# One inference step of a hybrid decoder: the query latents and the pool inputs of the front stage as seven half products per pair instead of eight

## What is computed

```
h = rms_norm(x, attn_norm)
z = h @ w_in                 # 2048 -> q_a 512 | ckv 256 | krope 64 | u 512 | qm 512 | gate 2048
q_a, ckv, krope, u, qm, gate = split(z)
kv = rms_norm(mem) @ w_mem_kv                       # 256 memory tokens -> 1024
mla   = attend(rms_norm(q_a) ..., rms_norm(ckv), rope(krope))   # prompt: causal; sample: paged cache
pool  = (mean of the last 2 / 4 / 8 / 16 rows of u, minus u) @ w_pool * pool_scale
cross = softmax(qm k) v
x = x + (concat[mla, pool, cross] * silu(gate)) @ w_out;  y = rms_norm(x)
```

## Time and profile before

| | before |
|---|---|
| median of 3 runs | 867.82 us (867.19 to 867.97) |
| profiled execution, span from first to last instruction | 865.3 us |
| profiled execution's own time | only its span is recorded; the median is 2.5 us above it |
| PE busy | 856.4 us (99%) |
| DVE / ACT / POOL busy | 590.4 / 464.5 / 147.4 us |
| DMA | 168.56 MB, mean 195 GB/s |

### The profile page before, as it was taken

One profiled execution on the slowest core, in us unless ns is written; L12 is line 12 of the kernel. 1 busy time (PEld: TensorE's weight loads), 2 busy tenths in 40 slices (PEclk: granted clock), 3 DMA queues, 4 the chain that ended last, 5 costly groups with the idle time before them and its releaser, 6 DMA issues.

```text
span 865.3 us, 15858 instructions
## 1 busy us (share of the span) xinstructions
PE 856.4 (99%) x5549; PEld 781.2 (90%) x5549; DVE 590.4 (68%) x1018; ACT 464.5 (54%) x774; POOL 147.4 (17%) x210
## 2 busy tenths in 40 slices
PE   9999999999999999999999999999999999999996
PEld 9999999999989999999999999888887788888885
DVE  6546635532349688888888875967678889563777
ACT  7665422122233566676667663577777546363446
POOL 0003001411300112323232331000000111111123
PEclk9999999999999999999999999999999999999998
DMA  9895435223364587878788754524127775988586
GB/s 357 303 290 208 134 134 182 73 85 103 102 256 182 175 275 245 253 256 248 250 254 251 250 172 136 220 86 159 37 97 299 165 213 115 257 218 262 118 156 218
DMA packets 64878, 168.56 MB, mean 195 GB/s; under 512 B 9672, under 2 KB 27657, under 8 KB 62808
## 3 DMA queue, kind: packets, MB, share of 16 engines
q1 hardware_dynamic: 52672, 126.46, 42.4%
q0 software_dynamic: 10752, 33.56, 16.9%
q10 hardware_dynamic: 1376, 7.54, 2.5%
...
## 4 chain that ended last, share of the span: by engine, by line
PE 99%; ACT 0%; issue 0%; DVE 0%; POOL 0%; ACTq 0%; DVEq 0%; POOLq 0%
...
## 5 line engine op out<-in xcount | busy, mean ns | idle before, releaser
L67 PE MATMUL z<-x_hi,w_hi 128*128 128x288 f32 x512 | 152.5, 298 | 0.0
L69 PE MATMUL z<-x_hi,w_lo 128*128 128x288 f32 x512 | 150.8, 294 | 0.0
L68 PE MATMUL z<-x_lo,w_hi 128*128 128x288 f32 x512 | 150.7, 294 | 0.0
L184 ACT ACTIVATE w_hi<-w_raw 128x1024 fp32r<-128x1024 f32 (+2 forms) x62 | 64.8, 1045 | 135.7 <-PE z L69 55.0
L191 DVE TENSOR_TENSOR w_lo<-w_raw,w_hi 128x1024 fp32r<-128x1024 f32 (+2 forms) x62 | 76.9, 1241 | 70.8 <-ACT w_hi L184 70.4
L1024 POOL DMA_DIRECT2D v_raw<-in_cache x128 | 69.3, 541 | 176.0 <-issue 174.4
L67 PEld LDWEIGHTS z<-x_hi,w_hi 128*128 128x128 f32 x512 | 96.1, 188 | 2.7 <-issue 1.1
L68 PEld LDWEIGHTS z<-x_lo,w_hi 128*128 128x128 f32 x512 | 96.1, 188 | 1.6 <-issue 0.2
L69 PEld LDWEIGHTS z<-x_hi,w_lo 128*128 128x128 f32 x512 | 96.0, 188 | 0.0
L2056 ACT ACTIVATE o_hi<-o_raw 128x1024 fp32r<-128x1024 f32 x50 | 52.9, 1060 | 71.1 <-PE pa_s L3030 38.1
L2310 DVE TENSOR_TENSOR o_lo<-o_raw,o_hi 128x1024 fp32r<-128x1024 f32 x50 | 60.9, 1220 | 34.6 <-ACT o_hi L2056 34.4
...
## 6 DMA issues: line engine op xcount, KB each, us to landing
w_raw<-in_w_feat SPq DMA_DIRECT2D x56, 512.0 KB, 4.0
k_raw<-in_cache SPq DMA_DIRECT2D x128, 192.0 KB, 3.1
v_raw<-in_cache POOLq DMA_DIRECT2D x128, 128.0 KB, 3.3
o_raw<-in_w_out POOLq DMA_DIRECT2D x30, 512.0 KB, 8.4
o_raw<-in_w_out SPq DMA_DIRECT2D x20, 512.0 KB, 8.5
w_raw<-in_w_mem_kv SPq DMA_DIRECT2D x16, 512.0 KB, 4.3
...
```

What stands on the lines that cost most here:

```text
L67: pe.matmul(out, a[0], b[0], start=start, stop=False, skip_group_check=onto)
L68: pe.matmul(out, a[0], b[1], start=False, stop=False, skip_group_check=onto)
L69: return pe.matmul(out, a[1], b[0], start=False, stop=stop, skip_group_check=onto)
L184: act.activation(hi_slot(s, u)[:, lo:w], s.wraw[:, u % RAW, lo:w], ACT.Copy).then_inc(s.w_hi, 1)
```

## The change

The eight tiles of q_a and u are taken out of the ring of units and computed ahead of the memory units, as four pairs of tiles. For a pair the product is a 2 x 2 by 2 x 2 product of blocks: two feature tiles by two halves of the inputs, times two halves of the inputs by two halves of the tokens. Directly that takes eight half products; the change uses seven (a form of Strassen's scheme), each of 24 matmuls of 288 columns, on sums of blocks. With a, b, c, d the four weight blocks of 128 x 1024 of a pair, the weight sums are X = c + d, Y = X - a, Z = b - Y and a - c; of x scaled by the norm's weights (`x_scaled`, four blocks f0 to f3 of 128 x 2304) the token sums are T1 = f1 - f0, T2 = f3 - T1, T3 = f3 - f1 and T4 = f2 - T2. The products are, in this order: X T1, Y T2, Z f3, (a - c) T3, a f0, d T4, b f2; their sums are put together by three copies on ACT and six additions on DVE for each pair.

- POOL, new: 13 instructions of 128 x 576 that make `x_scaled` (L494 of the changed kernel), while x arrives, and T3 (L500). ACT makes the other three tiles' upper blocks.
- DVE, new: T1, T2, T4 (L807, L811, L819), the low parts of T1 to T4 (L770), four weight sums for each pair (L721 to L748), the low part for each product (L763), the six additions.
- ACT, new: the high parts of T1 to T4 (L570) and of the weights of each of 28 products (L588), three ahead of PE.
- Then units in the order `ORDER`: the four pool gates' tiles and one tile of qm (numbered 0 to 4, units f0 to f9), mixed with the memory units m0 to m15. Before, two memory units and one feature unit alternated, and the gates came last.
- The work of the pool group moves into this stretch; at which unit each step stands is written in tables (`DIFF_AT`, `PO_AT`, `BEND_AT` and others, by the unit's place in `ORDER`).
- The later filling has 60 parts instead of 64 (the tile of qm went to the front); `LONG` loses the steps 6, 12, 18 and 24.

```diff
-FEATS, FRONT = 28, 12
+PGATE, GATE, QM = range(0, 4), range(5, 17), (4, 17, 18, 19)
+FEATS, FRONT = 20, 5
 BASE = KV_UNITS + MEM_UNITS
...
+FIRST = BASE + 2 * FRONT
...
+ORDER = [("f", 0), ("f", 1), ("m", 0), ("m", 1), ("m", 2), ("m", 3)]
+for n_ in range(2, 8):
+    ORDER += [("f", n_), ("m", 2 * n_), ("m", 2 * n_ + 1)]
+ORDER += [("f", 8), ("f", 9)]
...
+PAIRS, TERMS = 4, 7
+PRODUCTS = PAIRS * TERMS
...
+TERM_ROLE = "XYZcadb"
...
+ACT_F = 13
...
+Z_OUT_AT = {4: 0, 12: 1, 18: 2, 24: 3}
+DIFF_AT = {6: 0, 12: 1, 16: 2, 20: 3}
+PO_AT = {12: 0, 16: 1, 20: 2, 24: 3}
+BEND_AT = {9: 0, 16: 1, 19: 2, 25: 3}
+POOLED_AFTER = {9: 0, 13: 1, 17: 2, 20: 3}
...
+            for n in range(1, PAIRS):
+                done = TERMS * (n - 1)
+                if n == 1:
+                    sp.wait_ge(s.w_used, KV_UNITS)
+                else:
+                    sp.wait_ge(s.st_used, done)
+                sp.wait_ge(s12, 2 * n - 1)
+                pair_load(n, "c")
+                sp.wait_ge(s.st_used, done + 1)
+                pair_load(n, "d")
+                sp.wait_ge(s.st_used, done + 2)
+                pair_load(n, "a")
+                sp.wait_ge(s.st_used, done + 3)
+                pair_load(n, "b")
...
+            pool.wait_ge(gx0_in, 16)
+            for c, (k0, k1) in enumerate(X_CHUNKS):
+                pool.wait_ge(xt_landed[c], 16)
+                for k in range(k0, min(k1, ACT_F)):
+                    pool.tensor_scalar(fs[:, 2 * (k // 8):2 * (k // 8) + 2, k % 8, :], halves(xraw[:, k, :]), gx[:, k:k + 1], None,
+                                       ALU.mult).then_inc(scaled, 1)
...
+            pool.wait_ge(scaled, ACT_F)
+            pool.wait_ge(x_hi, 2 * KD - ACT_F)
+            pool.wait_ge(x_lo, KD)
+            pool.tensor_tensor(traw[:, 2, :, :], fs[:, 3, :, :], fs[:, 1, :, :], ALU.subtract).then_inc(s3, 1)
...
+                pool.wait_ge(u_ready, 3 * (g + 1))
...
+                pool.tensor_copy(by_seq(U(g))[:, :, 0:STATE], src).then_inc(prep, 1)
+                pool.wait_ge(prep, 2 + 2 * (g + 1))
+                if g:
                     pool.wait_ge(diff, g)
-                cur, nxt, other = U[:, g, :], s0, s1
...
+                v = gt[:, g, :]
                 pool.tensor_tensor(po[:, g, :], po[:, g, :], v, ALU.mult).then_inc(gated, 1)
                 pool.wait_ge(gated, 2 * g + 1)
                 pool.tensor_tensor(v, po[:, g, :], th[:], ALU.mult).then_inc(gated, 1)
...
+            def turned_hi(t):
+                if t != 3:
+                    act.wait_ge(t_sum, {1: 1, 2: 2, 4: 3}[t])
+                if t in (2, 3):
+                    act.wait_ge(s3, 1)
+                act.activation(t_high(t), traw[:, t - 1, :, :], ACT.Copy).then_inc(st_hi, 1)
...
+            def pair_hi(m):
...
+                if m < HI:
+                    act.wait_ge(s.w_used, m + 4)
+                else:
+                    act.wait_ge(s.st_used, m - HI + 1)
+                act.activation(high(s, m % HI), raw(n, role), ACT.Copy).then_inc(st_hi, 1)
...
+            turned_hi(1)
+            pair_hi(0)
+            square_row(0)
+            turned_hi(2)
+            pair_hi(1)
+            turned_hi(3)
+            pair_hi(2)
+            turned_hi(4)
...
+            for step in range(PRODUCTS):
+                n, i = divmod(step, TERMS)
...
+                        act.wait_ge(bc, 1)
+                        act.wait_ge(s.st_used, 22 - TERMS)
+                    name, dst = {0: ("C", target(n, 1, 1)), 1: ("B", target(n, 0, 1)), 4: ("A", target(n, 0, 0))}[i]
+                    act.activation(dst, sums_bank(n, name), ACT.Copy).then_inc(st_cp, 1)
+                if step + HI < PRODUCTS:
...
+                if j in BEND_AT:
+                    g = BEND_AT[j]
+                    act.wait_ge(z_out, g + 1)
                     if g:
                         act.wait_ge(gated, 2 * g)
-                    act.activation(th[:], gt[:, g % GT, :], ACT.Sigmoid).then_inc(bent, 1)
+                    act.activation(th[:], gt[:, g, :], ACT.Sigmoid).then_inc(bent, 1)
...
+            def first(n):
...
+                dve.tensor_tensor(raw(n, "X"), raw(n, "c"), raw(n, "d"), ALU.add).then_inc(s12, 1)
...
+            def second(n):
...
+                dve.tensor_tensor(raw(n, "Y"), raw(n, "X"), raw(n, "a"), ALU.subtract).then_inc(s12, 1)
...
+            def third(n):
...
+                dve.tensor_tensor(raw(n, "c"), raw(n, "a"), raw(n, "c"), ALU.subtract).then_inc(s3, 1)
...
+            def fourth(n):
...
+                dve.tensor_tensor(raw(n, "Z"), raw(n, "b"), raw(n, "Y"), ALU.subtract).then_inc(s4, 1)
...
+            def pair_lo(m):
...
+                if k == 12:
+                    dve.wait_ge(scaled, 8)
+                    dve.tensor_tensor(traw[:, 0, :, :], fs[:, 1, :, :], fs[:, 0, :, :], ALU.subtract).then_inc(t_sum, 1)
+            dve.wait_ge(scaled, ACT_F)
+            dve.wait_ge(x_hi, 2 * KD - ACT_F)
+            dve.wait_ge(t_sum, 1)
+            dve.tensor_tensor(traw[:, 1, :, :], fs[:, 3, :, :], traw[:, 0, :, :], ALU.subtract).then_inc(t_sum, 1)
+            first(0)
+            turned_lo(1)
+            second(0)
+            pair_lo(0)
+            fourth(0)
+            third(0)
+            dve.wait_ge(t_sum, 2)
+            dve.tensor_tensor(traw[:, 3, :, :], fs[:, 2, :, :], traw[:, 1, :, :], ALU.subtract).then_inc(t_sum, 1)
+            turned_lo(2)
+            pair_lo(1)
+            pair_lo(2)
+            turned_lo(3)
...
+                    dve.wait_ge(s.w_used, gate_unit(g) + 1)
...
+                    dve.tensor_tensor(halves(gt[:, g, :]), gate_sums, rbc[:], ALU.mult).then_inc(z_out, 1)
+                if j in PO_AT:
+                    g = PO_AT[j]
                     dve.wait_ge(pooled, g + 1)
...
+                if j in DIFF_AT:
+                    g = DIFF_AT[j]
                     dve.wait_ge(win, (g + 1) * (g + 2) // 2)
                     sm = (s0, s1)[g % 2]
                     if g:
                         dve.wait_ge(pooled, g)
...
+            def pair_product(m):
+                n, i = divmod(m, TERMS)
+                turned = {0: 1, 1: 2, 3: 3, 5: 4}
+                if i in turned:
+                    b = t_high(turned[i]), t_low(turned[i])
...
+                    b = {2: x_block(8, 1), 4: x_block(0, 0), 6: x_block(8, 0)}[i]
+                bank, start = {0: ("C", True), 1: ("B", True), 2: ("C", False), 3: ("B", False), 4: ("A", True), 5: ("B", False), 6: ("C", True)}[i]
...
+                pe.wait_ge(st_hi, hi_count(m))
+                pe.wait_ge(st_lo, lo_count(m))
+                w = high(s, m % HI), low(n, TERM_ROLE[i])
+                for kk in range(8):
+                    last = product(pe, sums_bank(n, bank), [v[:, P * kk:P * kk + P] for v in w],
+                                   (b[0][:, kk, :], b[1][:, kk, :]), start and kk == 0, kk == 7, not start)
+                last.then_inc(s.st_used, 1)
...
-LONG = (*range(2, 28, 2), STEPS - 1)
+LONG = (2, 4, 8, 10, 14, 16, 20, 22, 26, STEPS - 1)
...
+            dve.tensor_tensor(s.qm[:, 0, :].rearrange("p (a b) -> p a b", a=2), s.front_sums, rbc[:], ALU.mult).then_inc(qm0_out, 1)
...
```

771 lines of the change are left out of this document (462 added, 309 removed).

## The result

The changed kernel takes 884.23 us (median of 4 runs, 881.42 to 885.22) against 867.76 us (4 runs): 1.0187 times as long, 95% interval 1.0171 to 1.0203, or 16.5 us more. The profiled execution is the shortest of them, 881.42 us with a span of 879.7, so its trace accounts for 14.4 us only. The last experiment shows where most of the other 2.8 us sit.

A forecast was written before the change was run, and what follows sets the result against it. PE, busy 99% of the span, was taken to bound the kernel. 867.8 - 12.8 (matmuls saved) + 22 (start) + 8.5 (second sigmoid) + 3 (clock) = 888.5 us; range for 8 in 10, 868.5 to 898.

The forecast's parts named there:

- Saved on PE: Four pairs at the front: seven half products instead of eight, 96 matmuls less at 0.133 us each, 12.8 us gained.
- Added on DVE at the start: DVE's row of sums and low parts before the first two products: 8.3 us to each, 5.1 us of waiting as lower bound.
- POOL in DVE's way: At the start, 13 scalings (1.2 us each, 15.6) and T3 (4.45) add to DVE's time: second product at 64.8, 22 us lost.
- The second sigmoid: Ahead of m10, ACT's sigmoid waits for POOL's first gate, behind group 3's four window additions: 8.5 us lost, 7 to 10.
- The clock: PE waits longer than 4 us two or three times and restarts at a lower clock: 3 us for all, 0 to 6.
- The filling: Four of the 38 steps lose a part of 3.2 us; DVE still short of full: nothing, up to 3 us.
- The sum: Whole kernel: 867.8 - 12.8 + 22 + 8.5 + 3 = 888.5 us.
- Rival 1: At the start, POOL does not hold DVE up, scalings fall into DVE's gaps or leave the port free: 870.1 us, chance 0.15.
- Rivals 2 and 3: 2: the sigmoid's wait costs nothing, 880.0 us, chance 0.12; 3: only DVE's row waits at the second product, 860.1, chance 0.10.
- the gap at m10: Sign of being right: an 8 us gap on PE ahead of m10, released through ACT's w_hi behind the sigmoid.
- rival 4: On PE, more matmuls run than counted, not the seven products; PE's instruction list has 95 rows less; chance 0.01.
- the gaps of 10 and 5 us at the start: Sign of being right: PE gaps of some 10 and 5 us ahead of the first two half products.

The follow-up runs named there:

- The last experiment: The changed kernel run once more as it is, on the same chip, nothing changed: 884.13 us, ratio 1.0183; the profiled run took 884.85 us.

## Why the prediction was right and wrong

It said 888.5 us, in a range of 868.5 to 898, slower with 0.86; measured are 884.2. The direction and the mechanism hold: two chains on other queues, one at the start and one ahead of m10, and a clock that falls behind them. By its own steps:

- **Saved on PE**, 12.8 us: 96 matmuls went (5549 to 5453). The front ends 24.7 us late and the kernel 14.4, so 10.3 us of it arrive.
- **Added on DVE at the start**: right to 0.1 us an instruction (2.46 us for 2304 columns, 1.14 for 1024). From T2 to the second product the row and T3 were to take 16.7 + 4.45 = 21.2 us and took 22.3.
- **POOL in DVE's way**: here the prediction failed, by 8.5 us. The second product was put at 64.8 us and started at 56.35, so 13.5 us were lost and not 22. The step that failed is the price of a scaling as seen by VectorE: 1.2 us was taken, fully added to VectorE's time, and it was 0.42 us (0.46 by the run with three fewer), though the instruction itself takes 2.16 us on GpSimd. 13 x 0.42 = 5.4 us in place of 15.6 puts T2 at 28.0 + 5.4 = 33.4 us; it was at 34.08. I took a one-input instruction to shut VectorE out for as long as it runs, as a two-input one does. For the two-input T3 that is nearly what happened: 5.0 us, against 4.45 foretold, and the Trainium skill's rule of the exclusive lock (SBUF — State Buffer, Terms) agrees with it: 6.17 us beside it and 1.22 without. For the scalings that rule, by which the loser is blocked for the full instruction, is not borne out by the profile's durations: 0.42 us lost beside 2.16. The estimate from the Trainium skill's line rate (GPSIMD Engine Reference, Engine selection), 0.6 us, was nearer for VectorE's loss and far off for GpSimd's own time, of which the shortest was 1.72 us.
- **The second sigmoid**: 8.5 us foretold, 8.25 measured. The windows took 6.0 and not 7.75 us; VectorE was idle in those 6.0 us and busy for 3.9 in the 7.75 of before. In exchange VectorE's low part of m10 took 2.42 us beside GpSimd's next gate. Taking the order away gave 9.7 us back.
- **The clock**: 3 us for all, and it was 1.8 to 2.4 at m10 and, in most runs, some 2.4 at the start, so 4 to 5. How long TensorE stays at the lower level, which no row of before showed, the profiles of the changed kernel show: from m10's start at 221.29 us to 225.2 in the first, from 224.19 to 229.4 in the second.
- **The filling**: taken at nothing, range 3. The stretch behind the front gives back 10.3 instead of 12.8 us. 1.3 us of the 2.5 are waits for the keys' parts at four steps (three for VectorE's `k_lo`, one for ScalarE's `kr_hl`), which the prediction held covered; the other 1.1 are busy time of TensorE, which fell behind the front by 11.7 us and not 12.8, and why stays open. The parts can't simply be taken from the query stage, which needs them more (4.4 us lost).
- **The sum**, corrected by these: 888.5 - 8.5 + 1.5 + 2.5 = 884.0 us. That 888.5 came within 4.3 us is in part luck: an error of 8.5 us too much met two that came to 4 us too little.

Rival 1 had the scalings' harmlessness too strong but was right that they hurt little; its 870.1 fails by 8.4 us more at the start (56.35 against 47.9 us; 5.0 of it are T3 on GpSimd), by the clock and by the filling. Rivals 2 and 3 fall with the waits at m10 and at the start. Of the signs named, the gap at m10 came with its chain (8.25 us for 8), TensorE has 96 matmuls less (rival 4 counted 95), the gaps of 10 and 5 us at the start were 6.98 and 3.64, and the second product was at 56.35 us and not near 65.
